# Writing out the group loop and moving the turned queries and keys ahead of the third pair of convolution tiles

## What is computed

```python
u = rmsnorm(h, mix_pre_norm[l])
proj = u @ w_in[l]
q, k, v, z, xbc, dt_raw, g_a, g_b = _split(proj, IN_WIDTHS)
q = rope(q.reshape(b, s, ATTN_HEADS, HEAD_DIM), positions)
k = rope(k.reshape(b, s, ATTN_KV_HEADS, HEAD_DIM), positions)
v = v.reshape(b, s, ATTN_KV_HEADS, HEAD_DIM)
y_attn = banded_sink_attention(q, k, v, attn_sinks[l]) @ w_attn_out[l]
y_ssd = ssd_mixer(z, xbc, dt_raw, ssd_conv_w[l], ssd_conv_b[l], ssd_dt_bias[l],
                  ssd_a_log[l], ssd_d[l], ssd_norm[l]) @ w_ssd_out[l]
merged = jax.nn.sigmoid(g_a) * y_attn + jax.nn.sigmoid(g_b) * y_ssd
h = h + rmsnorm(merged @ w_out[l], mix_post_norm[l])
f = causal_dwconv(rmsnorm(h, ffn_pre_norm[l]) @ w_up[l], ffn_conv_w[l], ffn_conv_b[l])
f_gate, f_val = _split(f, (D_FF, D_FF))
h = h + rmsnorm((jax.nn.silu(f_gate) * f_val) @ w_down[l], ffn_post_norm[l])
```

## Time and profile before

| | before |
|---|---|
| median of 3 runs | 1100.73 us |
| the profiled execution: time | 1097.28 us |
| the profiled execution: span | 1095.5 us |
| TensorE (matmul) busy | 1060.7 us, 97% |
| VectorE busy | 656.6 us, 60% |
| ScalarE busy | 456.8 us, 42% |
| GpSimd busy | 132.2 us, 12% |
| mean granted TensorE clock | 0.988 of full |

### The profile page before, as it was taken

The page is one execution under the profiler, slowest core; times in us unless marked ns, Lnnn a source line. Parts: engine busy times, 40 slices in busy tenths (PEclk is TensorE's granted clock), DMA queues, the critical chain, the costliest instruction groups (busy, mean ns, idle before and its releaser), DMA issues.

```text
span 1095.5 us, 14663 instructions
## 1 busy us (share of the span) xinstructions
PE 1060.7 (97%) x5313; PEld 890.4 (81%) x5313; DVE 656.6 (60%) x943; ACT 456.8 (42%) x720; POOL 132.2 (12%) x200
## 2 busy tenths in 40 slices
PE   6999999989999999999999999999999999999997
PEld 6877887769778977888888888888888888888886
DVE  6877777775787678763242323367666666651214
ACT  6465346533654465452141213264343434331212
POOL 7103201320133013300000003020000000000001
PEclk8999999989999999999999999999999999999999
DMA  7321132113211321132323242512242424233221
GB/s 200 99 68 30 48 107 69 30 44 114 68 31 39 116 78 39 39 116 77 115 77 115 77 158 110 179 52 77 77 115 77 114 79 112 80 112 116 78 76 77
DMA packets 111608, 95.51 MB, mean 87 GB/s; under 512 B 15344, under 2 KB 101692, under 8 KB 111548
## 3 DMA queue, kind: packets, MB, share of 16 engines
q1 hardware_dynamic: 111547, 94.74, 28.4%
HBM read 92.63 MB, written 2.10 MB: 86 GB/s over the span
## 4 chain that ended last, share of the span: by engine, by line
PE 91%; ACT 3%; DVE 2%; issue 2%; DMA 1%; POOL 1%; SPq 0%; DVEq 0%; ACTq 0%; POOLq 0%
PE ps L1187 18%; PE ps L1185 18%; PE ps L1186 18%; PE ps L1192 9%; PE ps L1193 9%; PE ps L1194 9%; PE ps L1402 3%; PE ps L1350 1%; PE ps L1398 1%; PE ps L1414 1%; ACT qB L562 1%; PE ps L1423 1%; PE ps L1327 1%; DVE wlo L784 1%; PE ps L1328 1%
## 5 line engine op out<-in xcount | busy, mean ns | idle before, releaser
L784 DVE TENSOR_TENSOR wlo<-raw,whi 128x2048 fp32r<-128x2048 f32 (+1 forms) x83 | 187.0, 2255 | 219.9 <-ACT whi L440 219.9
L1185 PE MATMUL ps<-uhi,whi 128*128 128x512 f32 x640 | 249.3, 389 | 0.0
L1187 PE MATMUL ps<-uhi,wlo 128*128 128x512 f32 x640 | 249.1, 389 | 0.0
L1186 PE MATMUL ps<-ulo,whi 128*128 128x512 f32 x640 | 249.0, 389 | 0.0
L440 ACT ACTIVATE whi<-raw 128x2048 fp32r<-128x2048 f32 (+1 forms) x83 | 156.0, 1881 | 173.7 <-PE ps L1194 93.0
L1185 PEld LDWEIGHTS ps<-uhi,whi 128*128 128x128 f32 x640 | 120.1, 188 | 25.1 <-DVE wlo L784 0.2
L1187 PEld LDWEIGHTS ps<-uhi,wlo 128*128 128x128 f32 x640 | 120.1, 188 | 24.9
L1186 PEld LDWEIGHTS ps<-ulo,whi 128*128 128x128 f32 x640 | 120.1, 188 | 24.8
L1192 PE MATMUL ps<-whi,uhi 128*128 128x512 f32 (+1 forms) x320 | 124.0, 387 | 6.7 <-issue 4.7
L1193 PE MATMUL ps<-whi,ulo 128*128 128x512 f32 (+1 forms) x320 | 120.4, 376 | 0.0
L1194 PE MATMUL ps<-wlo,uhi 128*128 128x512 f32 (+1 forms) x320 | 120.3, 376 | 0.0
(11 more groups left out here) (225 smaller groups left out, 1463.4 us busy)
## 6 DMA issues: line engine op xcount, KB each, us to landing
raw<-in_w_in_dram SPq DMA_DIRECT2D x24, 1024.0 KB
raw<-in_w_up_dram SPq DMA_DIRECT2D x44, 512.0 KB
raw<-in_w_down_dram SPq DMA_DIRECT2D x11, 1024.0 KB
raw<-in_w_in_dram SPq DMA_DIRECT2D x16, 512.0 KB
raw<-in_w_ssd_out_dram SPq DMA_DIRECT2D x8, 1024.0 KB
raw<-in_w_attn_out_dram SPq DMA_DIRECT2D x4, 1024.0 KB
raw<-in_w_out_dram SPq DMA_DIRECT2D x4, 1024.0 KB
yT<-in_x_dram SPq DMA_DIRECT2D x4, 512.0 KB, 4.6
```

The lines of the kernel that those rows point to most:

```text
L784: dve.tensor_tensor(wlo[sl][:, 0:width] if into is None else into, raw[sl][:, 0:width], h.bitcast(F32), ALU.subtract).then_inc(s["lo_done" ...
L1185: pe.matmul(bank(b)[:, span], hi_[:, k, c], ah[:, span], start=first and k == 0, stop=False)
L1186: pe.matmul(bank(b)[:, span], hi_[:, k, c], al[:, span], start=False, stop=False)
L1187: ins = pe.matmul(bank(b)[:, span], lo_[:, k, c], ah[:, span], start=False, stop=last and k == KD - 1)
```

## The change

Two things are changed. The loop over pairs of groups is written out as four calls on TensorE, ScalarE, VectorE and GpSimd, so that every wait value and address of the groups is a constant. And on TensorE the block of turned queries and keys and decay sums moves from behind `conv_tiles(4)` to ahead of it. On ScalarE their evictions and the exponential of the decays go right behind `tap(3)`, ahead of `build(0)`, with `tanh(2)` between them.

```diff
@@ gpsimd, scalar, vector (with its link counts) and tensor alike
-            with pool.Fori(0, NG // 2) as i:
-                group(i, 0)
-                group(i, 1)
+            for G in range(NG):
+                group(*divmod(G, 2))
@@ scalar, in group
                 tap(3)
-                act.wait_ge(s["dt_ok"], G + 1)
-                act.wait_ge(s["seg_mm"], G * 2 * NT)
-                build(0)
-                tanh(2)
-                hi_next(4)
-                tap(4)
-                tanh(3)
-                tap(5)
                 def halves(a):
                     return a.rearrange("p (t b c) -> p t b c", b=2, c=HD)
...
                                ACT.Copy).then_inc(s["qkT_sb"], 1)
+                tanh(2)
                 act.wait_ge(s["decay_mm"], G + 1)
                 act.activation(dec[:, :, :, :].rearrange("p a t h -> p (a t h)"), bank(3, 3 * NT * SH), ACT.Exp).then_inc(s["decay_ok"], 1)
+                act.wait_ge(s["dt_ok"], G + 1)
+                act.wait_ge(s["seg_mm"], G * 2 * NT)
+                build(0)
+                hi_next(4)
+                tap(4)
+                tanh(3)
+                tap(5)
                 tok(0)
                 tanh(4)
                 tanh(5)
@@ tensor, in group
                 conv_tiles(2)
                 conv_tiles(3)
-                conv_tiles(4)
                 pe.wait_ge(s["qkv_sb"], G * NT + NT)
                 pe.wait_ge(s["roped"], G * NT + NT)
...
                 ins.then_inc(s["decay_mm"], 1)
+
+                conv_tiles(4)
```

More of the change, by code:

```diff
@@ L621, in group @@
                 hi_next(7, BLK if p else 4 * QKV)
-            with act.Fori(0, NG // 2) as i:
-                group(i, 0)
-                group(i, 1)
+            for G in range(NG):
+                group(*divmod(G, 2))
             act.wait_ge(s["o_sb"], NG * NT)
@@ L842, in _ @@
             link(dve.tensor_scalar(hp[:, 1, :], hp[:, 1, :], -1.0, None, ALU.mult))
-            before = links["n"]
             def group(i, p):
@@ L1424, in group @@
                     ins.then_inc(s["o_mm"], 1)
-            with pe.Fori(0, NG // 2) as i:
-                group(i, 0)
-                group(i, 1)
+            for G in range(NG):
+                group(*divmod(G, 2))
             pe.wait_ge(s["zg_ok"], NG * NT)
@@ L1585, in bass_f32_inverse @@
     return np.float32(1.0) / np.float32(ROPE_THETA ** (2.0 * k / width))
-PAIR_LINKS = 150
 _INS = ['x', 'positions', 'mix_pre_norm', 'w_in', 'attn_sinks', 'ssd_conv_w', 'ssd_conv_b', 'ssd_dt_bias',
```

## The result

The changed kernel takes 1090.99 us (median of 4 runs, 1089.89 to 1092.66), the kernel before 1100.68 us in the same comparison: a ratio of 0.9916, 95% interval 0.9898 to 0.9934, or 9.7 us less. It was compared twice more in the experiments, at 0.9938 (0.9924 to 0.9952) and 0.9937 (0.9918 to 0.9955), 7 us less each time. The forecast of 8.0 us less, 1092.7 us, lies between the three.

A forecast was written before the change was run, and what follows sets the result against it. TensorE, busy 97% of the span, was taken as the bound, so only its waits and lower clock pay. Gains of 6.7 and 3.85 less 2.55 us make 8.0: 1092.7 us from 1100.73, range 1088.5 to 1098.5.

The forecast's parts named there:

- Part 1: Writing out the loop removes TensorE's idle time and low-clock matmuls between groups 1 and 2: 6.7 us gained.
- Part 2: Moving the block of turned queries and keys: 3.85 us gained over four groups, less 2.55 us for the lower clock.
- the chain: ScalarE and VectorE queue from hi_next(4) to lo_next(5): z starts 1.1 us earlier in group 1, 3.85 us over four.
- the clock: 1.2 GHz behind TensorE's new idle stretch: 0 to 1.7 us a group, taken as 0.85 in three of four, 2.55 us.
- constants for register values: Constants in wait values and addresses shorten the sequencers' work, not seen on the path: 0, at most 1 us gained.
- the other engines' branches: Loop branches of the other three engines lie beside TensorE's: worth nothing more.
- part 1 is worth only the branch instruction itself: Reading by the skill's 108 ns compare-and-branch at the loop's end: an estimated 0.1 us gained; no chance given.
- rival 3: The 4.72 us are code fetch, and TensorE still waits for the second copy: 1099.4 us; chance 0.07.
- the new wait: TensorE idles in tok(2) for the eviction of tok(1) behind hi_next(5), 2.2 us, and some 0.4 behind tok(4).
- Rival 2: The clock falls in all four groups wholly on z, 1.7 us each: 1097.0 us; chance 0.15.
- Rival 4: GpSimd's segments slow VectorE in taps(5), 2.0 us more per group, making it slower: 1105.0 us; chance 0.05.
- The scale: The median before, 1100.73 us, lay 3.45 above the profiled execution; the forecast is put on the median's scale.

The follow-up runs named there:

- b4: The kernel before, unchanged, run again for a second profile: 0.9992 of the kernel before.
- b2: The kernel before with only the block moved, the loop over pairs kept on all engines: 0.9989 of the kernel before.
- b1: The changed kernel with the block put back, so only the loop written out on all four engines: 0.9918 of the kernel before.
- c5: The kernel before with TensorE's loop alone written out and nothing moved: 0.9930 of the kernel before.
- c1: The changed kernel with hi_next(4) put right behind tap(3), ahead of the evictions: 0.9875 of the kernel before.
- d2: The changed kernel with 10 filler matmuls per group in TensorE's idle time, result unused: 1087.44 us, 0.9894 of the kernel before.
- b3: The changed kernel, unchanged, run again beside the two parts on one chip: 0.9938 of the kernel before.
- d3: The changed kernel, unchanged, run again on the filler kernel's chip: 1092.11 us, 0.9937 of the kernel before.
- b: The comparison on one chip of written-out loop alone (0.9918), move alone (0.9989), changed kernel (0.9938) and kernel before (0.9992).
- c3: The changed kernel with the eviction of tok(1) put right behind tok(0), ahead of tanh(4) and hi_next(5): 0.9952 of the kernel before.
- d1: The c2 kernel with x times dt of token tile 0 ahead of the softmax on VectorE: 0.9847 of the kernel before.
- c2: The changed kernel with ScalarE and VectorE reordered around the moved block, hi_next(4) and tanh(2) behind tap(3): 0.9869 of the kernel before.

## Why the prediction was right, and where it was off

The time and the direction were right: 8.0 us forecast, 9.7, 6.8 and 7.0 measured. Part 1 was right by its mechanism. Part 2 had the chain right and the clock too cheap, so that on top of the written-out loop it is a loss and not a gain; that the sum came out so near is luck. By its steps:

- **Part 1, 6.7 us.** In the traces 6.75 us between the two first profiles; the boundary of b4 and b2 is longer by 0.2 and 0.75 us than the first one's before. So the pair of boundaries without and with a branch was the right ruler. Alone the part measured 9.0 (7.5 to 10.6) on all engines and 7.7 (6.0 to 9.4) on TensorE alone. What the sum left at 0, constants for register values, brings nothing on the ruler where the clock stays up. What differs on the ruler is the time at 1.2 GHz inside the groups, from 25 us of the span on and the boundary left out: 10.2 and 13.7 us in the two profiles before, 6.8 in b1 and in c5. That the constants cause this is not shown, with two profiles on each side. That the other engines' branches are worth nothing fits c5.
- **That part 1 is worth only the branch instruction itself** (0.1 us, near rival 3's 1099.4) is refuted: the idle time was 4.5 to 4.8 us in each of the three profiles with the loop on TensorE, and no profile without it shows such idle time. Nor does idle time without a releaser of over 0.4 us stand in the groups of the written-out kernels, so rival 3 falls. The one exception is the first matmul of group 0 (at 17 us of the span: the groups begin there and not at 27 us): TensorE waits 1.0 to 1.9 us for it in every profile, with the loop or without, and in three of them no releaser is named. That the 4.7 us are the fetch of code is argued and not shown: the profile names no releaser.
- **Part 2, the chain.** Right at each station (above), and so was its point, that the move gains less than the 2.1 us of the waits, since `hi_next(4)` is queued behind the evictions. With the clock held up by the filler, z starts 23.2 us behind E, where the forecast has 22.98. c1 shows that this queue was the cause: one call put ahead lets z start 1.0 us earlier in each group, with 6.9 us by the ratios.
- **Part 2, the new wait.** Forecast 2.2 and 0.4 us; 2.61 and, at the lower clock, none. At the full clock (d2) the second is 0.34 us, for the eviction of the next `tok` (L507) and not for `lo`. TensorE was through the scores at 185.7 and not 186.0.
- **The term that was mis-sized is the clock.** I took 0.85 us in three of four groups, 2.55 us. In the first profile after it fell in all four, and in two further profiles (b3, d3) in three; the spared group reads 26.0 there, and so do all groups of d2. Against 26.0 the groups where it fell lose 0.8 to 1.3 us each, 3.4 to 4.1 us in all. Of the difference to the forecast's 25.85 (z at 22.98 and 2.87 for its 12 matmuls), some 0.15 us a group is not the clock but z, 0.2 us later than the chain gave it. Rival 2 had the clock down in all four groups, as the first profile has it, but at 1.7 us a group.
- **Where the luck lies.** Part 2 alone is a loss of 0.9 us in the first pair of traces and about 2 us in b3 against b1, where I had a gain of 1.3. Two errors of opposite sign met: in b, part 1 was 2.3 us better than 6.7 and part 2 3.5 us worse than a gain of 1.3, and 8.0 + 2.3 - 3.5 = 6.8 is what b3 measured. These differences of times are each good to about 2 us. In the loop (b2 against before) part 2 measured 1.2 us of gain (0.2 to 2.3), too little to be told from nothing, though close to the 1.3 forecast; its trace has the clock down in all four groups. Why it does better there is not shown.
- **Rival 4** did not occur: `taps(5)` stayed at 2.31 us with GpSimd beside it, and the two products with the decays came down from 2.53 to 1.29 us, as forecast.
- **The scale.** The first profiled execution was 3.45 us below the median before, and b4's was as slow as that median. Of the 3.5 us between these two, 2.0 stand on the ruler: 3.4 us at 1.2 GHz in each of groups 0, 1 and 3 in the first, 6.8 us in each of groups 1 and 3 in b4. That this is also what moves the medians, and with them the three comparisons of the changed kernel, is likely but not shown. Why the clock falls in some groups of an execution, and for 3.4 or 6.8 us, stays open.

## What to carry to other kernels

Before moving evictions to where they are covered, list what they are now ahead of in the same engine's queue, and follow that to the next thing TensorE waits for: here a rounding delayed by 4.2 us set the next wait, and one call put back ahead of the evictions was worth 6.9 us by the ratios, nearly as much as the written-out loop. Price an idle stretch of TensorE with the matmuls behind it, too, and see whether its pieces come together into one. A wait that the trace names may hide another of about its length: c3 and d1 each removed the one named and met the next.

## What the runs showed of the hardware

- TensorE's branch back over the body of two groups left it idle for 4.50 to 4.82 us in all three profiles of kernels with that loop on TensorE, and 12, 17 and 15 matmuls behind it ran at 1.2 GHz (0.33 us apart where 0.18 is usual). The loops of the later parts, with shorter bodies, show no such idle time. The Trainium skill ("Runtime: NRT & Kernel Launch", Instruction fetch mechanics) has the fetch stall of a taken branch, without a figure; the trace agrees with a stall there, and does not show that it is the fetch.
- Idle time of 1.6 and 0.3 us around 1.5 us of transposes (c1) left the clock up behind them in all four groups. 2.6 us in one piece brought it down in 4, 3 and 3 of 4 groups in the three profiles of the changed kernel, 2.5 us in 4 of 4 in b2, and 3.1 us in 4 of 4 in c3. With the old order, 2.2 us in three pieces brought it down in 3 and 2 of 4 groups in the two profiles before, and 2.0 us in three pieces in 2 of 4 in b1 and in c5. Adding 10 matmuls whose result is not used (d2) made a group about 1 us shorter.
- VectorE is slowed beside GpSimd in some instructions and not in others. `lo`, with both inputs in SBUF, took 2.92 us in c2 with GpSimd's segments beside its first 0.8 us, against 2.29; the products with the decays 2.53 against 1.29; the taps, with one input in PSUM, 2.31 with and without. The row of c2:

```profile
179.94 2.92 DVE L782 TENSOR_TENSOR wlo<-raw,whi 128x2048 fp32r<-128x2048 f32 x1
```

The Trainium skill ("GPSIMD Engine Reference", Specifications) names contention with VectorE instructions that have two SBUF inputs; these three agree.
